# A hybrid encoder block on one core: convolution by token halves, weight splits on VectorE, gate products inside the attention

## What is computed

```
h = x @ W_in + b_in        # [conv a,gate: 2*512 | q,k,v: 3*512 | gates: 2*1024]
y_conv = silu(LayerNorm(causal_depthwise_conv31(a * sigmoid(gate)))) @ W_pw2 + b_pw2
y_sb   = stick_breaking_attention(q, k, v) @ W_o       # 8 heads of 64, strictly causal
mix    = (sigmoid(g_A) * y_conv + sigmoid(g_B) * y_sb) @ W_out + b_out
x      = LayerNorm(2**0.25 * x + mix)
y_peer = PEER(x)     # 8 heads, product keys 128 x 128, top 16, rows gathered from u and v
x      = LayerNorm(2**0.25 * x + y_peer)
```

## Time and profile before

| | |
|---|---|
| median of 3 runs | 3286.3 us (3282.34 to 3288.89) |
| profiled execution, its own time | 3283.15 us |
| its span from first to last instruction | 3281.3 us |
| busy: PE / DVE / ACT / POOL | 2446.8 / 2297.7 / 1159.3 / 1326.3 us |
| mean granted clock of PE | 0.864 of full |
| DMA in the expert part | 409 GB/s |

### The profile page before, as it was taken

The page is one execution under the profiler, slowest core; times in us unless marked ns, Lnnn a source line. Parts: engine busy times, 40 slices in busy tenths (PEclk is TensorE's granted clock), DMA queues, the critical chain, the costliest instruction groups (busy, mean ns, idle before and its releaser), DMA issues. The chain is left out here.

```text
span 3281.3 us, 37294 instructions
## 1 busy us (share of the span) xinstructions
PE 2446.8 (75%) x12464; PEld 998.8 (30%) x12464; DVE 2297.7 (70%) x4704; ACT 1159.3 (35%) x3326; POOL 1326.3 (40%) x1197
## 2 busy tenths in 40 slices
PE   8987996778778777769899888885555555555555
PEld 7864653332223333323233332221111111111111
DVE  6986215776668888876667866666777677767775
ACT  3106112333334555533333333333333333333332
POOL 3400003344445544544343344444455445444553
PEclk9998997888888898889999999997777777777777
DMA  3101226999999999999999999999999999999997
GB/s 142 39 0 65 77 104 272 396 413 420 421 420 405 410 409 375 409 420 410 397 397 419 394 409 412 421 419 421 409 421 421 420 398 421 421 421 402 421 421 313
DMA packets 162792, 1163.71 MB, mean 355 GB/s; under 512 B 17857, under 2 KB 17985, under 8 KB 26178
## 3 DMA queue, kind: packets, MB, share of 16 engines
q0 software_dynamic: 147456, 1073.81, 79.7%
q1 hardware_dynamic: 15170, 87.79, 6.8%
HBM read 1157.33 MB, written 4.19 MB: 354 GB/s over the span
## 5 line engine op out<-in xcount | busy, mean ns | idle before, releaser
L809 PE MATMUL ps<-arena_high 64*64 64x512 f32 x8192 | 1275.3, 749 | 724.2 <-ACT arena_high L1163 721.2
L590 POOL DMA_INDIRECT arena_high<-uv_dram,idx_now x1024 | 1201.8, 1174 | 1468.7 <-PE ps L809 1269.4
L1486 DVE SCALAR_TENSOR_TENSOR arena_high<-arena_low,arena_high 128x1024 f32<-128x1024 f32 x1024 | 1237.2, 1224 | 631.4 <-DMA arena_high<-uv_dram,idx_now 620.8
L809 PEld LDWEIGHTS ps<-arena_high 64*64 64x64 f32 x8192 | 308.3, 156 | 1567.7 <-ACT arena_high L1163 1101.6
L1154 ACT ACTIVATE gcol<-hcol 128x2 f32<-128x2 f32 x512 | 103.7, 202 | 1405.8 <-DVE arena_high L1486 1403.7
L1163 ACT ACTIVATE arena_high<-arena_high,wcol 128x64 f32<-128x64 f32 x1024 | 300.4, 340 | 16.7
L1156 ACT ACTIVATE wcol<-gcol,arena_high 128x1 f32<-128x1 f32 x1024 | 245.7, 287 | 16.8
L778 PE MATMUL ps<-arena_low 128*128 128x512 f32 (+1 forms) x512 | 223.5, 580 | 0.0
L1331 DVE SCALAR_TENSOR_TENSOR arena_low<-arena_high,cols,arena_low 128x1024 f32<-128x1024 f32 x120 | 183.9, 1533 | 4.3
L585 POOL CAST idx_now<-arena_high 128x8 uint32<-128x8 f32 x128 | 59.0, 461 | 255.3 <-DVE arena_high L1472 254.7
L211 PE MATMUL ps<-x_hi_bytes,w_bytes 128*128 128x512 f32 x384 | 151.0, 393 | 0.0
(11 more groups left out here) (169 smaller groups left out, 2476.4 us busy)
## 6 DMA issues: line engine op xcount, KB each, us to landing
arena_low<-slabs_dram SPq DMA_DIRECT2D x21, 1152.0 KB
arena_high<-uv_dram,idx_now POOLq DMA_INDIRECT x1024
arena_high<-w_mix_dram SPq DMA_DIRECT2D x8, 1536.0 KB, 6.8
arena_low<-w_mix_dram SPq DMA_DIRECT2D x8, 1536.0 KB
arena_high<-w_proj_dram SPq DMA_DIRECT2D x16, 512.0 KB, 3.5
arena_high<-xT_dram SPq DMA_DIRECT2D x8, 512.0 KB, 7.7
arena_high<-w_out_dram SPq DMA_DIRECT2D x2, 2048.0 KB, 11.1
arena_high<-x_dram SPq DMA_DIRECT2D x8, 512.0 KB, 7.8
```

The costliest lines, as they stand in the source:

```text
L590: pool.indirect_dma_start(out=ring[:, s % RING, :], out_offset=None, in_=uv_d, in_offset=bass.IndirectOffsetOnAxis(ap=idx_now[:, s:s + 1], ...
L809: last = nc.tensor.matmul(ps[out_rows, bank, :], diag[rows, s % DIAGS, :], ring[rows, s % RING, cs], start=False, stop=False, skip_group_c ...
L1486: last = nc.vector.scalar_tensor_tensor(out=ring[:, s % RING, 0:D], in0=x1[c][:, j, :], scalar=1.0, in1=ring[:, s % RING, 0:D], op0=ALU.mu ...
```

## The change

- **Slab order**: the eight a and gate slabs first, then four q, then four k.
- **Convolution by halves**: a gated product and 31 taps are now issued for half h=1 of a tile (512 tokens), for all four tiles; then for h=0 of tiles 0, 1 and 2. Two gated products per tile write the two halves' inputs (the late one keeps 30 tokens more). The 31 taps of tile 3, half 0, are issued inside the attention, two after each head's product.
- **Splits on DVE**: all 16 slab splits, among the taps, and the eight of the value weights after the taps of tile 0, half 0. POOL has none left.
- **Statistics by halves**: mean, variance, root, reciprocal and swish of h=1 run between value blocks; those of h=0 in units 10 to 14 of the attention.
- **Gates in the attention**: each unit starts with one group of 24 gate products, in banks 6 and 7. Scores, transposes and values now have one pair of banks each. The gates' sigmoids are stored; only branch products and mixing come after the attention, with three pairs of banks and weights loaded four deep in transfers of their own. W_out's second half and two rows are loaded sooner.

Its core:

```diff
 # GpSimd: the loops over w1_rounded and wv_rounded with their 24 subtractions are gone
 # PE
-            for b in range(6):
+            value_block(0)
+            pe.wait_ge(conv_done, CC)
+            conv_mean(1, 4)
+            value_block(1)
+            value_block(2)
+            value_block(3)
+            conv_var(1, 5)
+            for b in range(4, NB):
                 value_block(b)
...
-                if n >= 2:
-                    pe.wait_ge(beta_done, 2 * n - 2)
+                if n >= 1:
+                    pe.wait_ge(beta_done, 2 * n)
...
+            def gate_group(n):
+                m, g = n // 2, n % 2
+                pe.wait_ge(w_split, n + 1)
+                if n >= 2:
+                    pe.wait_ge(sigs_ready, n - 1)
+                for k in range(KD):
+                    ws = slice(g * D + k * P, g * D + (k + 1) * P)
+                    last = split_products(ps[:, 6 + g, :], (w_hi_r[:, m % 2, ws], w_lo_r[:, m % 2, ws]),
+                                          (x_hi_r[:, 0, k, :], x_lo_r[:, 0, k, :]), k == 0, k == KD - 1)
+                last.then_inc(gates_done, 1)
             scores_of(0)
             for n in range(NU):
+                gate_group(n)
+                if n == 10:
+                    pe.wait_ge(conv_done, 2 * CC)
+                    pe.wait_ge(out_read, 2)
+                    conv_mean(0, 5)
+                if n == 11:
+                    pe.wait_ge(centred, 2 * CC)
+                    conv_var(0, 5)
+                turn_weights(n)
                 if n + 1 < NU:
                     scores_of(n + 1)
-                turn_weights(n)
                 if n >= 1:
                     values_of(n - 1)
 # ACT, in the attention
             for n in range(NU):
+                gate_sigmoid(n)
+                if n == 11:
+                    conv_squares(0)
+                if n == 12:
+                    conv_std(0, 5)
+                if n == 14:
+                    conv_swish(0)
+                for hd in range(2):
+                    weights_out(n, hd)
                 for hd in range(2):
                     if n + 1 < NU:
                         stick_sigmoids(n + 1, hd)
-                    weights_out(n, hd)
+                if n % 2 == 1 and n // 2 + 2 < KD:
+                    round_w(n // 2 + 2)
 # DVE
+            glu(0)
             for c in range(CC):
+                for k in range(TAPS):
+                    i = c * TAPS + k
+                    if i % 13 == 4 and i // 13 < 8:
+                        split_w1(4 + i // 13)
+                    conv_tap(taps_done, c, 1, k)
+                    if c == 0 and k == TAPS - 1:
+                        glu(1)
+                    if c in (1, 2) and k == TAPS // 2:
+                        glu(c + 1)
+            for k in range(TAPS):
+                if k % 8 == 0:
+                    split_w1(12 + k // 8)
+                conv_tap(taps_done, 0, 0, k)
+            for k in range(KD):
+                dve.wait_ge(wv_rounded, k + 1)
...
+            for k in range(TAPS):
+                conv_tap(taps_done, 1, 0, k)
+            for k in range(TAPS):
+                conv_tap(taps_done, 2, 0, k)
+                if k == 8:
+                    conv_centre(1, 4)
+            split_gates(0)
+            conv_scale(1)
+            split_gates(1)
...
             for n in range(NU):
                 for hd in range(2):
                     break_stick(n, hd)
+                    for k in range(4 * n + 2 * hd, min(4 * n + 2 * hd + 2, TAPS)):
+                        conv_tap(taps_done, 3, 0, k)
+                if n % 2 == 0 and 2 <= n <= 12:
+                    split_gates(n // 2 + 1)
+                if n == 10:
+                    conv_centre(0, 5)
+                if n == 13:
+                    conv_scale(0)
 # order of the slabs
-        order += [c * P, CONV + c * P, col_q + c * P, col_k + c * P]
+        order += [c * P, CONV + c * P]
+    order += [col_q + c * P for c in range(CC)] + [col_k + c * P for c in range(CC)]
```

More of the change, by code:

```diff
@@ L552, in _ @@
             ones_where(ident64, P // 2, -P // 2).then_inc(consts, 1)
[L555 to L567, removed]
             pool.wait_ge(v_done, NB)
@@ new lines, in _ @@
+            for it in range(2):
+                next_w1(it, 0)
+                gate_out(2 * it)
+                next_w1(it, 1)
+                next_w1(it, 2)
+                gate_out(2 * it + 1)
+                next_w1(it, 3)
+            for c in range(CC):
+                act.wait_ge(proj_done, 2 * CC + c + 1)
+                nc.scalar.activation(q_both(c), halves(ps_flat[:, 2 * c * HALF:(2 * c + 2) * HALF]), ACT.Identity,
+                                     bias=q_bias8[:, c:c + 1], scale=DH ** -0.5).then_inc(psum_read[c], 1)
+                next_w1(2, c)
@@ L1021, in _, with round_w @@
-            for c in range(CC):
-                projected(c)
+            for c in range(CC):
+                act.wait_ge(proj_done, 3 * CC + c + 1)
+                nc.scalar.activation(kT[:, c, :], ps_flat[:, 2 * c * HALF:(2 * c + 2) * HALF], ACT.Identity,
+                                     bias=cols[:, C_K + c:C_K + c + 1]).then_inc(psum_read[c], 1)
+            def round_w(m):
+                act.wait_ge(wgate_in[m % 2], (m // 2 + 1) * 16)
+                for g in range(2):
+                    nc.scalar.activation(w_hi_r[:, m % 2, g * D:(g + 1) * D], w_gate[:, m % 2, g * D:(g + 1) * D],
+                                         ACT.Copy).then_inc(w_rounded, 1)
@@ L1349, in _, with conv_tap @@
-            dve.wait_ge(normed, CC)
+            dve.wait_ge(pad_ready, 2)
+            def conv_tap(steps, c, h, k):
+                tap = c * TAPS + C_CW + k
+                src = conv_in[:, c % 2, :] if h == 1 else conv_in_late[:, c, :]
+                src = src[:, PAD - k:PAD - k + HALF]
+                out = conv_h[h][:, c, :]
+                if k == 0:
+                    ins = nc.vector.tensor_scalar(out, src, cols[:, tap:tap + 1], cols[:, C_CB + c:C_CB + c + 1],
+                                                  ALU.mult, ALU.add)
+                else:
+                    ins = nc.vector.scalar_tensor_tensor(out=out, in0=src, scalar=cols[:, tap:tap + 1], in1=out,
+                                                         op0=ALU.mult, op1=ALU.add)
+                if k < TAPS - 1:
+                    steps.link(ins)
+                else:
+                    ins.then_inc(conv_done, 1)
@@ new lines, in conv_centre, with conv_scale @@
+            def conv_centre(h, bank):
+                dve.wait_ge(conv_done, CC * (2 - h))
+                dve.wait_ge(mean_done, 2 - h)
+                for c in range(CC):
+                    nc.vector.tensor_tensor(conv_h[h][:, c, :], conv_h[h][:, c, :], ps[:, bank, :],
+                                            ALU.subtract).then_inc(centred, 1)
+            def conv_scale(h):
+                dve.wait_ge(std_done, 2 - h)
+                nc.vector.reciprocal(rstd_row[h], rstd_row[h]).then_inc(rstd_done, 1)
+                dve.wait_ge(rstd_done, 2 - h)
+                dve.wait_ge(centred, CC * (2 - h))
+                for c in range(CC):
+                    nc.vector.tensor_tensor(conv_h[h][:, c, :], conv_h[h][:, c, :], rstd_row[h], ALU.mult).then_inc(normed, 1)
```

316 lines of the change are left out of this document (151 added, 165 removed).

## The result

The change makes the kernel faster: **3255.0 us** median (3250.9 to 3259.0, 4 runs) against 3287.6 us for the kernel before on the same chip (3282.3 to 3289.4, 4 runs), ratio 0.990 [0.989, 0.992]. The profiled execution took 3253.66 us with a span of 3251.6, against 3283.15 and 3281.3 before. In what follows "after" is the changed kernel, and L... are its lines unless said otherwise.

A forecast was written before the change was run, and what follows sets the result against it. PE, with gaps waiting on VectorE, bounded the stages before the DMA-limited expert part. Saving 15.4 us before the attention and 9.4 after its start gave 24.8, so 3261 us, range 3245 to 3275 for 8 in 10 runs.

The forecast's parts named there:

- Narrow taps: VectorE's convolution: a tap of 512 elements starts every 0.787 us, bounds 0.68 and 1.32.
- Rival 1: Ahead of slab 12: taps up to 0.72 us, so no new wait; 36.6 us gained, 3250 us; chance 0.12.
- rival 3: Ahead of the attention: narrow taps do not shrink, deciding from about 0.95 us a tap; 3370 us; chance 0.03.
- Earlier start: Projection start: VectorE's first subtractions on x meet no GpSimd work, so PE's first matmul comes 1 us earlier (0 to 1).
- The new wait: Ahead of slab 12, the first k slab: PE waits 8.4 us for VectorE's split, issued after four tile halves.
- Half clock behind it: After the gap ahead of slab 12: PE runs at 1.2 instead of 2.4 GHz, losing 3.4 us (0 to 5).
- PE ready for the attention: End of value blocks and h=1 statistics: PE is ready at 260.1 instead of 275.5 us.
- VectorE ready, 11 us to spare: Before the attention: VectorE's work is done at about 246 to 249 us, 11 us ahead of PE.
- Attention with gates: Attention: PE's work, gates included, sets 130.5 us, plus 5 of waits (0 to 15): 135.5, ending at 395.6.
- Rival 2: Attention: single score banks chain the engines, nothing overlaps; 145 us, 9.5 more, 3271 us in all; chance 0.14.
- Rival 4: Expert part: limited by DMA, it stretches by what it starts earlier, so no gain; 3284 us; chance 0.06.
- The long taps: Convolution before the change: three rows of 30 taps were 29.7 us too long, only while GpSimd subtracted twelve times.

The follow-up runs named there:

- the second execution: The changed kernel run once more with no edit, beside the others on the same chip: 3255.9 us, ratio 0.990 against the kernel before.

## Why the prediction was right, point by point

- **Narrow taps** (0.787 us): measured 0.788. Rival 1's 0.72 and rival 3's 0.95 both fall.
- **Earlier start** (1 us): 1.5 us (9.57 to 8.08), partly since the first weight rounding began 0.6 us earlier. The size was right, its working was not. Of the subtractions on x only the longest (2.18 us), beside GpSimd's split, was stretched, and the median was 1.22. The mean of 1.33 us over seven is the pace of ScalarE, whose roundings of x began 1.35 us apart. Slab 11 ended at 140.98; forecast 142.0.
- **The new wait** (8.4 us): right in kind, place and name, 5.3 us in size. The failing terms are VectorE's. It began at 33.50 instead of 35.95. I had moved its start by PE's 1 us alone, and the gate slab ended 2.1 us earlier. Another 1.28 us is a table load of ScalarE, which stood between the gate slab's end and its sigmoid before and now lies ahead of the slab's end (rows below). The eight splits took 1.14 instead of 1.26 each, 1.0 us; tile halves and gated products gave 0.9. Together these are 4.3 us for the split of slab 12 (144.81, forecast 149.1), less the 1.0 that PE came earlier.

ScalarE of the kernel before, and then of after, in order of time:

```profile
34.32 1.28 ACT L1008 ACT_TABLE_LOAD   x1 [5.44 <-PE ps L211]
35.61 1.12 ACT L1008 ACTIVATE arena_high<-ps,cols 128x1024 f32<-128x1024 f32 x1
```

```profile
26.74 1.28 ACT L1026 ACT_TABLE_LOAD   x1
32.23 1.12 ACT L1026 ACTIVATE arena_high<-ps,cols 128x1024 f32<-128x1024 f32 x1 [4.21 <-PE ps L212]
```

- **Half clock behind it** (3.4 us): 1.4. Six products started every 0.45 us instead of 0.227 (146.27 to 148.97). The loss behind a gap of 9 us did not carry over to one of 5. On the other side is a loss of 1.5 that I had not counted, six slow products and a slow bias behind the 1.30 us eviction wait (192.68 to 196.63).
- **PE ready for the attention** (260.1): 255.7. The 4.4 are 1.0 + 3.1 + 2.0 of the three steps above, less 1.7 in the value blocks (63.0 us, forecast 61.6, and rounding).
- **VectorE ready, 11 us to spare**: the kernel with the taps moved ahead gives 15.
- **Attention with gates** (135.5, of it 130.5 PE's own and 5 of waits): 134.2, of it 130.6 busy and 3.6 idle, at a clock of 1.00. VectorE 85 (forecast 90), ScalarE 70 (69). The waits named were the first sigmoid (none), the mean's bank (none seen), the variance (L642, 1.4) and the tail (0.9). Rival 2, nothing overlaps, falls: without the gates inside, the whole is 64 us slower. Its price of 145 us was too low as well, since it gave the attention 12 us per head pair, and this order without the gates takes 108.6 us, or 101 with idle products.
- **Branches** (54.9 us, end 450.5): 55.2, end 445.1.
- **Expert part as long as before**: 2806.5 against 2806.0. Rival 4 falls. DMA share and rate from 700 us on are the same, 1.00 and 409 GB/s.
- **The long taps** (29.7 us beside twelve subtractions of GpSimd): the twelve are not all. The eight splits of the value weights ran under the third row of 30 taps, the one of 50.91 us. So some 20 splits stood beside the long taps, and on VectorE they would have cost 12 x 1.14 + 8 x 0.60 = 18.5 us.

GpSimd of the kernel before, three splits while VectorE rested, and then the eight of the value weights:

```profile
18.30 7.12 POOL L557 TENSOR_TENSOR w_bytes<-arena_high,w_hi_bytes 128x1024 fp32r<-128x1024 f32 x3 [9.95 <-ACT w_hi_bytes L981]
...
151.15 17.89 POOL L566 TENSOR_TENSOR w_bytes<-arena_high,w_bytes 128x512 fp32r<-128x512 f32 x8
```

The sum was 24.8 us and the landmarks show 30.2 (28.8 in the second execution). Of the 5.4 between, 4.4 lie before the attention, 1.3 in it, and the branches take 0.3 back. Rival 1's outcome (no new wait) did not come, but the kernel with slab 12's split moved shows its price: the 7.8 us that it gained stand against the 11.8 I had put on it.

No run undoes the slab order, the convolution by halves, the statistics by halves or the deeper weight loads by itself. That the two gaps of 9 us went because of the halves is read from the timelines, and supported by the runs in which moving the splits alone removed only the first gap, and moving the taps ahead brought the second back.

Both sides of the gates' place are larger than the forecast let one see. Gates inside are worth 64 us against gates behind in the same order (medians on two chips; 62 to 64 by the landmarks), but that order (one pair of score banks, taps and the statistics of h=0 between the heads) has itself an attention of 108.6 us. The last product of the attention before, in order of time:

```profile
327.47 0.88 PE L685 MATMUL ps<-arena_low 128*64 128x128 f32 x12
```

It began at 275.5 and ended at 328.4, so 53 us. By the landmarks, first score to last branch product took 199.8 us before, 251.5 with the gates behind (257.1 to 508.6) and 189.4 after. So the change gives up 51.7 us for an order in which the gates can hide, and takes 62.1 back. The forecast had only the difference, 9.4, and that came out at 10.4.

## What to carry to other kernels

Where engines wait on each other in turn, put independent TensorE work in the chain before shortening it: 87 us of products went in for 33 us of time, and the first of them more than paid for themselves by keeping the clock up. When work moves from one engine to another, ask what reads its result at which time, and place each piece by its own due time: one split 14 taps too late cost 7.8 us, a quarter of what the whole change gained. Test a change of several parts by undoing one part in the new kernel and doing it alone in the old; here the same move was worth 0 in the one and 8 us in the other.

## What the runs showed of the hardware that was not expected

- Added TensorE work shortened a stretch: granted clock 0.58 without it, 0.90 with 21.8 us of it and 0.98 with 43.5, and 108.6, 101.4 and 101.9 us.
- The loss of clock behind a gap is not one price. After 8.99 us it was 3.4 us, after 5.29 us 1.4 us, and after only 1.30 us (at 192.68) there were again 1.5 us at half clock.
- GpSimd's splits and VectorE's taps disturb each other both ways. A split of 1024 elements took 7.12 / 3 = 2.37 us on GpSimd while VectorE rested, 2.91 on the mean beside the taps of the kernel before, and 1.22 on VectorE. The taps lost more than VectorE needs for the same work: 28.3 us beside 19 splits in the changed kernel (VectorE: 11 x 1.14 + 8 x 0.60 = 17.3) and 29.7 us beside some 20 in the kernel before (18.5).
